# A hybrid decoder block on one core: x loaded in four halves, norm gains turned ahead of it, gated scores behind the keys' transposes

## The reference

```
h     = rms_norm(x, norm1_gain)
proj  = h @ w_in            # gq gk | gv | gr | g_low (16) | mq | mk | mv
gate  = log_sigmoid(g_low @ w_gate_up + b_gate) / 16
o_gla = chunked gated linear attention(gq, gk, gv, gate)      # 4 heads, key 64, value 128
o_gla = rms_norm(o_gla, gla_out_gain) * silu(gr)
o_moba= causal attention(rotary(mq), rotary(mk), mv)          # 4 heads of 128, one block of 256 keys
o_moba= rms_norm(o_moba, moba_out_gain)
x     = x + concat(o_gla, o_moba) @ w_out
h     = rms_norm(x, norm2_gain)
x     = x + (silu(h @ w_ffn_gate) * (h @ w_ffn_up)) @ w_ffn_down      # d_ff = 2816
out   = rms_norm(x, final_norm_gain)
```

## Time and profile before

| | us |
|---|---|
| median of 3 runs | 300.39 (299.89 to 300.57) |
| the profiled execution | 300.49 |
| its span | 298.8 |
| PE busy | 292.5 (98%) |
| DVE busy | 240.4 (80%) |
| ACT busy | 172.4 (58%) |
| mean granted clock of TensorE | 0.996 |

### The profile page before, as it was taken

The page is one execution under the profiler, slowest core; times in us unless marked ns, Lnnn a source line. Parts: engine busy times, 40 slices in busy tenths (PEclk is TensorE's granted clock), DMA queues, the critical chain, the costliest instruction groups (busy, mean ns, idle before and its releaser), DMA issues.

```text
span 298.8 us, 4025 instructions
## 1 busy us (share of the span) xinstructions
PE 292.5 (98%) x1373; PEld 241.3 (81%) x1373; DVE 240.4 (80%) x401; ACT 172.4 (58%) x247; POOL 17.8 (6%) x40
## 2 busy tenths in 40 slices
PE   8999999999999999999999999999999999999992
PEld 6778888888898888887888888888888888888882
DVE  1999999777889687988888888979797978787155
ACT  3997799868765897717170808080808081713224
POOL 5120100000031001300000000000000000000002
PEclk9999999999999999999999999999999999999998
DMA  7997846737768122392929292919191919030003
GB/s 244 323 343 253 268 138 231 228 122 275 257 190 262 49 95 65 104 326 88 334 75 347 70 354 57 356 46 375 43 370 44 374 48 368 28 138 0 0 0 140
DMA packets 37382, 55.49 MB, mean 186 GB/s; under 512 B 2982, under 2 KB 26618, under 8 KB 37370
## 3 DMA queue, kind: packets, MB, share of 16 engines
q1 hardware_dynamic: 37204, 55.16, 54.9%
q10 hardware_dynamic: 166, 0.17, 0.2%
HBM read 53.75 MB, written 1.57 MB: 185 GB/s over the span
## 4 chain that ended last, share of the span: by engine, by line
PE 98%; DVE 0%; ACT 0%; issue 0%; DVEq 0%
PE acc L510 15%; PE acc L512 15%; PE acc L511 15%; PE aux L512 13%; PE aux L511 13%; PE aux L510 13%; PE aux L613 1%; PE acc L564 1%; PE acc L570 1%; PE acc L567 1%; PE acc L527 1%; PE aux L535 1%; PE aux L683 1%; PE aux L707 1%; PE aux L665 1%; PE aux L650 0%
## 5 line engine op out<-in xcount | busy, mean ns | idle before, releaser
L1153 DVE TENSOR_TENSOR w_lo<-raw,w_hi 128x2048 fp32r<-128x2048 f32 x46 | 103.4, 2286 | 16.0 <-ACT w_hi L879 15.9
L879 ACT CAST w_hi<-raw 128x2048 fp32r<-128x2048 f32 x46 | 85.9, 1908 | 4.7 <-DMA raw<-in_w_ffn_up 2.6
L510 PE MATMUL aux<-w_hi,aT_hi 128*128 128x512 f32 (+1 forms) x180 | 69.7, 387 | 0.0
L512 PE MATMUL aux<-w_hi,aT_lo 128*128 128x512 f32 (+1 forms) x180 | 69.6, 387 | 0.0
L511 PE MATMUL aux<-w_lo,aT_hi 128*128 128x512 f32 (+1 forms) x180 | 69.6, 387 | 0.0
L1455 DVE STREAM_TRANSPOSE reuse_c<-reuse_c 32x128 f32<-32x128 f32 x160 | 48.4, 303 | 2.4
L1091 ACT CAST pT_hi<-reuse_c 128x512 fp32r<-128x512 f32 x10 | 6.2, 621 | 72.8 <-DVE reuse_c L1455 72.8
L510 PE MATMUL acc<-w_hi,aT_hi 128*128 128x512 f32 x118 | 47.1, 399 | 0.0
L512 PE MATMUL acc<-w_hi,aT_lo 128*128 128x512 f32 x118 | 46.0, 390 | 0.0
L511 PE MATMUL acc<-w_lo,aT_hi 128*128 128x512 f32 x118 | 46.0, 390 | 0.0
L510 PEld LDWEIGHTS aux<-w_hi,aT_hi 128*128 128x128 f32 x180 | 33.8, 188 | 7.0
(11 more groups left out here) (204 smaller groups left out, 282.2 us busy)
## 6 DMA issues: line engine op xcount, KB each, us to landing
raw<-in_w_ffn_gate SPq DMA_DIRECT2D x22, 512.0 KB, 4.1
raw<-in_w_ffn_up SPq DMA_DIRECT2D x22, 512.0 KB, 5.3
raw<-in_w_ffn_down SPq DMA_DIRECT2D x22, 512.0 KB, 5.9
raw<-in_w_in SPq DMA_DIRECT2D x20, 512.0 KB, 4.7
raw<-in_w_out SPq DMA_DIRECT2D x8, 512.0 KB, 4.4
raw<-in_w_in SPq DMA_DIRECT2D x8, 256.0 KB, 5.3
x_sb<-in_x SPq DMA_DIRECT2D x2, 512.0 KB, 3.9
m_moves<-reuse_c SPq DMA_DIRECT2D x1, 512.0 KB, 3.2
```

The costliest lines, as they stand in the source:

```text
L510: nc.tensor.matmul(dst, left_hi[:, k, tok], right_hi, start=first, stop=False)
L512: return nc.tensor.matmul(dst, left_lo[:, k, tok], right_hi, start=False, stop=last)
L879: nc.scalar.copy(w_hi[:, slot % RING, :], raw[:, slot % RAW, :]).then_inc(hi_ready, 1)
L1153: nc.vector.tensor_tensor(w_lo[:, slot % RING, :], raw[:, slot % RAW, :], w_hi[:, slot % RING, :].bitcast(f32), ALU.subtract).then_inc(lo_ ...
```

## The change

The load of x is issued as four DMAs, each of one tile and one half of its columns, with a semaphore each; SyncE's wait ahead of the remaining first pieces, and ACT's wait ahead of the squares of tile 0, become waits for both halves. PE runs 11 warm-up matmuls instead of 16, turns the norm gains first, and then turns x a half at a time, in the old order of chunks, with the frequencies' transpose still between the tiles. `gla_scores` moves from the end of unit 7 to its middle, right behind `moba_k_transposed`.

```diff
--- before.py
+++ after.py
@@ -208,7 +208,7 @@
         ang, turns, turns_lo, sin_arg = (reuse_e[:, n * T * HALF:(n + 1) * T * HALF] for n in range(4))
 
 
-        x_loaded = [sem(f"x_loaded_{t}") for t in range(T)]
+        x_loaded = [[sem(f"x{t}_{side}_loaded") for side in ("left", "right")] for t in range(T)]
         rows_loaded = sem("rows_loaded")
         norm1_loaded = sem("norm1_loaded")
         low_loaded = sem("low_loaded")
@@ -334,10 +334,15 @@
                 sp.dma_start(raw[:, n // 4, (n % 4) * 512:(n % 4 + 1) * 512],
                              w_in[0, n * P:(n + 1) * P, BLOCKS[0]:BLOCKS[0] + 512]).then_inc(first_loaded[n], 16)
 
+            def load_x(t, h):
+                sp.dma_start(x_sb[:, t, h * 512:h * 512 + 512], x[0, t * P:(t + 1) * P, h * 512:h * 512 + 512]).then_inc(x_loaded[t][h], 16)
+
             for t in range(T):
-                sp.dma_start(x_sb[:, t, :], x[0, t * P:(t + 1) * P, :]).then_inc(x_loaded[t], 16)
+                for h in range(2):
+                    load_x(t, h)
             load_first(0)
-            sp.wait_ge(x_loaded[0], 16)
+            sp.wait_ge(x_loaded[0][0], 16)
+            sp.wait_ge(x_loaded[0][1], 16)
             for n in range(1, KC):
                 load_first(n)
 
@@ -526,7 +531,7 @@
                 for _ in range(n):
                     nc.tensor.matmul(acc[:, 2, 0:SEQ], warm[:, 0:P], warm, start=True, stop=True)
 
-            warm_up(16)
+            warm_up(11)
             pe.wait_ge(ident_built, 1)
 
             def x_transposed(t, banks):
@@ -537,15 +542,19 @@
                     if t == T - 1:
                         last.then_inc(xT_in_psum, 1)
 
-            pe.wait_ge(x_loaded[0], 16)
-            x_transposed(0, range(4))
+            def x_half_transposed(t, h):
+                pe.wait_ge(x_loaded[t][h], 16)
+                x_transposed(t, (2 * h, 2 * h + 1))
+
             pe.wait_ge(norm1_loaded, 16)
             nc.tensor.transpose(acc[:, 3, NORM1_ROW:NORM1_ROW + KC], gain_rows[0:KC, :],
                                 ident[0:KC, 0:KC]).then_inc(gains_in_psum, 1)
+            x_half_transposed(0, 0)
+            x_half_transposed(0, 1)
             pe.wait_ge(freq_loaded, 16)
             nc.tensor.transpose(acc[0:HALF, 0, 0:1], freq_row, ident[0:1, 0:1]).then_inc(freq_in_psum, 1)
-            pe.wait_ge(x_loaded[1], 16)
-            x_transposed(1, range(4))
+            x_half_transposed(1, 0)
+            x_half_transposed(1, 1)
             pe.wait_ge(gains_ready, 1)
             pe.wait_ge(freq_ready, 1)
 
@@ -785,9 +794,9 @@
                 down((slot + 2) % RING, j, first=first)
 
 
-            midway = {2: [logits], 7: [moba_k_transposed], 8: [moba_scores],
+            midway = {2: [logits], 7: [moba_k_transposed, gla_scores], 8: [moba_scores],
                       9: [probs_transposed], 10: [moba_outputs, gla_updates], 11: [gla_outputs, lambda: heads_transposed(0, (3, 0))]}
-            after = {3: [cumulate], 7: [gla_scores]}
+            after = {3: [cumulate]}
             for k in range(KC):
                 first_row(k)
                 if k == 0:
@@ -908,7 +917,8 @@
                 nc.scalar.copy(w_hi[:, n // 4, cols], raw[:, n // 4, cols]).then_inc(first_hi_ready, 1)
 
 
-            act.wait_ge(x_loaded[0], 16)
+            for loaded in x_loaded[0]:
+                act.wait_ge(loaded, 16)
             sum_squares(0, 0)
             act.wait_ge(gains_ready, 1)
             take_xT((0, 1))
```

## The result

| | before | after |
|---|---|---|
| median of 10 runs, us | 300.15 (299.70 to 300.57) | 301.11 (300.67 to 302.49) |
| ratio | | 1.0035, 95% interval 1.0025 to 1.0045 |
| the profiled execution | 300.49 | 300.91 |
| its span | 298.8 | 299.2 |

The kernel became slower, by 1.05 us in the ratio. The profiled execution of after is one of its faster ones and that of before one of its slower ones; the pair shows 0.42 of the loss.

The account below looks back on a forecast made before the run. The prediction took PE to bound the kernel. From the profiled 300.49, 0.55 off for the start and 0.0 for the join gave 299.94, beside 299.84 from the median; forecast 299.9 us, range 299.4 to 301.2.

Parts of the forecast that it names:

- What bounds the kernel, and where a gain would have to come from: Whole kernel: PE bounds it, busy 292.5 of 298.8 us; only time taken from PE's row or its loose start pays.
- The halves' landings: Start: halves of x land at about 3.65, 4.3, 5.0 and 5.65; weights delayed by nothing to 0.15 us.
- Rival 2: Start: weights bound it; x in 2 KB rows delays w_in, gain shrinks to 0.1 or 0.2, 300.3 us; chance 0.22.
- The clock: PE's start: the clock rises at 6.4 as before, so tile 1's transposes run four at 0.21 and four at 0.11.
- rival 1: PE's start: clock rises later after fewer warm-ups and more idle; 301.14 us for a rise at about 10; chance 0.27.
- The other form: PE's start, late clock: the Trainium skill says transposes do not count as busy, so the full clock does not engage.
- The norm gains first: PE's start: the gains' transpose hides in the gap between the warm-ups' end, near 3.35, and the first half of x.
- The join: Unit 7: gated scores put behind the keys' transposes remove no change of mode; 0.0, bounds minus 0.3 to plus 0.2.
- The delayed second half: Unit 7: twelve products behind the moved scores come 1.29 later, hidden by ACT's 1.35 idle, 0.06 to spare; counted as nothing.
- Covers: Unit 2 and rotated keys: PE has 0.78 and 0.98 to spare; a 0.55 gain fits, one over 0.75 would not.
- half loads: Start: x in four half loads lets PE transpose earlier; with gains first and fewer warm-ups, gain 0.55, bounds zero to 0.7.
- 11 warm-ups: PE's start: eleven warm-ups end near 3.35, so PE is free before the first half lands at about 3.65.

Follow-up runs that it names:

- e4: Kernel before with x in four half loads, 16 warm-ups and the gains' transpose in its old place: 300.61 us, ratio 1.0022.
- e9: Kernel before with a small load of 128 rows of 64 bytes behind each whole tile of x: 301.05 us, ratio 1.0045.
- e12: Kernel before with tile 0 of x in two half loads and tile 1 whole: 301.05 us, ratio 1.0034.
- e14: Kernel before with two small loads of 128 rows of 64 bytes, both behind tile 1 of x: 300.24 us, ratio 1.0004.
- e8: Kernel before with x in two loads, each the half rows of one side of both tiles: single execution, 301.48 us.
- e11: Kernel before with only the norm gains' transpose moved ahead of x, 16 warm-ups: 300.18 us, ratio 1.0004.
- e2: Kernel before with 11 warm-up matmuls in place of 16, nothing else changed: 301.65 us, ratio 1.0050.
- e3: Kernel before with gla_scores moved behind moba_k_transposed, nothing else changed: 299.93 us, ratio 0.9999.
- e5: Kernel before with 11 warm-up matmuls and five transposes of the identity behind them, in place of 16 warm-ups: 300.30 us, ratio 1.0006.
- e1: Changed kernel with 16 warm-up matmuls in place of 11: 300.69 us, ratio 1.0023.
- e10: Kernel before with 14 warm-ups, then the gains' and frequencies' transposes ahead of x, in whole loads: 300.33 us, ratio 1.0017.
- e15: Kernel before with 16 warm-ups, then the gains' and frequencies' transposes ahead of x, in whole loads: 299.92 us, ratio 0.9991.

## Why the prediction was wrong, point by point

**What bounds the kernel, and where a gain would have to come from.** Right. The 0.43 by which PE is late at the second row stands unchanged at the end.

**The halves' landings.** Wrong, and the larger error. The step took the loads as one stream cut at other places: "0.63 a half", weights later by "nothing to 0.15 us". Only the first half came in time (3.5). The second landed at 4.8, the third at 5.5, the last at 6.6 instead of 5.65, the weights at 7.2 instead of 6.35. So the second half holds PE's first eight transposes up by 0.41 (2.35 for 1.94), and where the clock is up early, as in e4, PE waits for the weights. e4 measures the whole at 0.66 us. SyncE's wait for both halves of tile 0 also ended half a microsecond late, and the low-rank weights were issued at 8.05 instead of 7.51, where the prediction kept everything "within 0.1". Rival 2 had the place and the sign for the first weights, and the right witness (a wait of DVE for them), but at a smaller size (6.8 for DVE, where it was 7.23): it let the gain shrink, not turn. Its other witness failed: ACT's wait for the fourth row of w_in did not grow from 0.74, it was 0.16.

**What makes the hole.** Open. I had blamed shorter rows. As such they are no slower: from 2.5 to 3.5 after moves 362 GB/s in 2 KB rows, before 365 in 4 KB rows. e9 has a hole without any 2 KB row of x, e12 has at least the whole loss with half of them, and e14 refutes the number of loads. What is regular is where the hole lies: from 3.5 to 4.5 the four profiled executions with x in four halves have 176 to 278 GB/s, the seven with loads as in before 398 to 434. One would like to read it as a third load that is not ready to move data until some 2.5 us after its issue, so that short first loads leave a hole ahead of it. The traces do not bear that out. In e12 the third load, tile 1, was issued at 1.71, and its first packet (only it has 4 KB rows there) moved at 3.45, 1.7 later. In e8 the dip from 2.5 to 3.5 lies inside the first load, which lands at 4.8; in e11 the hole comes 2.8 us and more after the third one's issue. And the DMA engines are not without work in the hole: their busy share is 0.80 in after and 1.01 in e9. In after 11 of the 86 packets of 2 KB that start from 3.5 to 4.5 take over 250 ns, where the usual one takes 84; in the microsecond before it is 4 of 176. What holds them is not shown.

**The clock.** The forecast stood on a rise at 6.4 "as before". In after it rose later in the profiled execution: the eight transposes to 7.95 and the first product pair are on the lower level. The first clock record of each trace gives the time: 6.41 in before, 8.67 in after, 10.34 in e2, but also 5.36 in e3, whose start is that of before. So the rise at 6.4 is not a property of the kernel but of the execution that was read; with an earlier one PE comes to the loads sooner, and their delay shows in full (e4). This is rival 1, with its place, and its mechanism in the better of the two forms I gave: the idle time. The other form, that transposes are not activity, is refuted by e5. So the section on PE-mode transposes of the Trainium skill's "TensorE: Matmul & The Clock Gate", which I had set beside rival 1, does not hold for these float32 transposes; 1.5 us were at stake, and e5 lost none that its interval tells from nothing. The price that rival 1 put on a rise at about 10, 1.2, was about right: e2's second row starts 1.26 after that of before. What it had wrong was how often: on the median of the changed kernel the shorter warm-up costs some 0.36 (e1), loosely known. That the rise comes late in only some of its executions is argued from this, not shown. Where the idle time is in one piece of 0.8, the median loses 1.5 (e2).

**The norm gains first.** Right that they hide: e11, 0.1 within its error.

**The join.** Right at 0.0, for the reason given: the trace after has the drain on the way out (0.43) as before, and the transposes and scores ahead of it take the same 0.87 and 1.09. e3 agrees. The delayed second half also went as worked out: ACT waits 1.34 for unit 7's end and has no idle time left before the exponentials, which start as soon as before relative to PE.

**Covers.** The change had no gain to carry, but e5's profiled execution tests them: its second row starts 0.93 before that of before, and its span is 1.0 shorter. The prediction held that a gain of over 0.75 would not fit, since DVE does not move with PE. DVE moved: unit 2's low part was complete 0.78 earlier, at 19.02, PE came at 19.65, and nothing was lost.

**The sum.** 299.9 came of -0.55 for the start; the start was worth +1.05. Of this, 0.66 is the term "half loads" mis-sized and 0.36 the term "11 warm-ups" put at nothing. That the measured 301.11 lies next to rival 1's 301.14 is luck: rival 1 reached it by the clock alone, and two thirds of the loss are the loads.

## What to carry to other kernels

Cutting a load so that its first piece can be used early pays only if its last piece, and what is queued behind it, land no later: read the landings of all of them and the rate in the windows view, not only the first piece. Here small loads were cheap behind the long ones and dear between them (e14, e9). A profile shows one execution; where its start differs from its siblings' by the time of a clock rise, forecast from more than one. When a warm-up is shortened to end as data arrives, count the idle tenths that it opens and fill them with anything, transposes included; and look at the single runs, not only the median, since a late clock shows as a second group of times.

## What the runs showed of the hardware that I had not expected

Five float32 transposes kept TensorE's clock on its way up as well as five matmuls did (e5: 1.0006, against 1.0050 for e2 with nothing in their place). An idle wait of 0.30 us, in a stretch otherwise nearly full, went with two groups of runs 1.4 us apart (e10), and with the wait filled the upper group was gone (e15). Two loads of 8 KB each cost 1.3 us in one place of the queue and 0.1 in another (e9, e14). The granted clock in the windows and on the page read 1.0 from the start, also while a 512-column pair took 1.05 us (e2) in place of 0.62; in these traces that figure is not to be trusted ahead of the first clock record (10.34 in e2), and the spacing of like instructions is.
